# First attention of a two-block model: 32 written-out rounds with the compressed branch and the turning of heads in pieces between them, first queries staged early

## The reference, cut to what matters

```python
def nsa_attention(q, gates, k_cmp, v_cmp, k_sel, v_sel, k_win, v_win, rel_bias):
    ...
        logit_c = jnp.einsum('bqghd,bngd->bqghn', qt, k_cmp) + bias_c[None]   # 31 compressed blocks
        p_c = jax.nn.softmax(logit_c, axis=-1) * has_any[...]
        o_c = jnp.einsum('bqghn,bngd->bqghd', p_c, v_cmp)
        ...
        logit_s = jnp.einsum('bqghd,bqgkd->bqghk', qt, ks) + bias_s           # selected blocks
        ...
        logit_w = jnp.einsum('bqghd,bkgd->bqghk', qt, kw) + bias_w[None]      # window of 512
        ...
        o = gt[..., 0:1] * o_c + gt[..., 1:2] * o_s + gt[..., 2:3] * o_w
    ...
def nsa_mixer(h, w_qg, w_o, shared, rel_bias):
    ...
    return o.reshape(B, S, N_HEADS * HEAD_DIM) @ w_o
```

## Time and profile before

| | |
|---|---|
| median of 3 runs | 2545.89 us (2544.61 to 2548.26) |
| the profiled execution's own time | 2548.19 us |
| its span, first to last instruction | 2546.3 us |
| PE busy | 2435.9 us (96%) |
| DVE busy | 1550.6 us (61%) |
| ACT busy | 875.4 us (34%) |
| POOL busy | 60.2 us (2%) |
| mean granted PE clock | 0.978 of 2.4 GHz |
| chain that ended last | PE 86%, DVE 7%, issue 4%, ACT 2%, DMA 1% |

### The profile page before, as it was taken

How to read it: one execution, slowest core, us unless ns; L and a number is a source line. 1 busy time by engine, 2 the same in 40 slices (tenths; PEclk the granted TensorE clock), 3 DMA queues, 4 the chain that set the end, 5 groups by cost and what they waited for, 6 DMA issues and landing times.

```text
span 2546.3 us, 38807 instructions
## 1 busy us (share of the span) xinstructions
PE 2435.9 (96%) x14805; PEld 2141.5 (84%) x14805; DVE 1550.6 (61%) x2803; ACT 875.4 (34%) x1343; POOL 60.2 (2%) x55
## 2 busy tenths in 40 slices
PE   6999999999989899999999989998998999999998
PEld 4888888888878788888878889988997999997996
DVE  5556444456477756344468875876665655884784
ACT  3123222234344443222244761673332333222222
POOL 0000000000112000000000000000100000000000
PEclk9999999999989899999999999999999999999999
DMA  4236224324433002222223422431221122223223
GB/s 141 89 99 149 88 99 144 122 99 126 150 104 71 21 29 92 91 100 96 86 99 101 122 63 84 118 100 67 83 83 65 64 84 84 83 99 128 87 84 115
DMA packets 91769, 242.42 MB, mean 95 GB/s; under 512 B 24886, under 2 KB 58166, under 8 KB 67638
## 3 DMA queue, kind: packets, MB, share of 16 engines
q1 hardware_dynamic: 29056, 198.26, 21.6%
q10 hardware_dynamic: 60808, 36.42, 6.4%
q0 software_dynamic: 1760, 5.77, 1.0%
HBM read 230.51 MB, written 11.14 MB: 95 GB/s over the span
## 4 chain that ended last, share of the span: by engine, by line
PE 86%; DVE 7%; issue 4%; ACT 2%; DMA 1%; ACTq 0%; DVEq 0%
PE ps L972 42%; PE ps L1208 24%; PE ps L1461 4%; PE ps L1309 3%; PE ps L1161 3%; PE ps L1106 1%; PE ps L1144 1%; DVE wlo L1478 1%; PE ps L1394 1%; PE ps L1065 1%; PE ps L1368 1%; DMA buckets<-in_buckets 1%; PE ps L992 1%; PE ps L1133 1%; ACT L L817 1%
## 5 line engine op out<-in xcount | busy, mean ns | idle before, releaser
L522 ACT ACTIVATE whi<-raw 128x2048 fp32r<-128x2048 f32 x187 | 357.6, 1912 | 731.9 <-PE ps L972 495.1
L1478 DVE TENSOR_TENSOR wlo<-raw,whi 128x2048 fp32r<-128x2048 f32 (+1 forms) x207 | 430.6, 2080 | 66.1 <-ACT whi L522 65.2
L972 PE MATMUL ps<-parts,whi 128*128 128x512 f32 x1360 | 429.7, 397 | 0.0
L1208 PE MATMUL ps<-parts,whi 128*128 128x264 f32 (+1 forms) x2400 | 409.9, 293 | 10.9 <-DVE sq L2109 5.6
L1208 PEld LDWEIGHTS ps<-parts,whi 128*128 128x128 f32 x2400 | 335.1, 191 | 22.7 <-issue 16.9
L972 PEld LDWEIGHTS ps<-parts,whi 128*128 128x128 f32 x1360 | 255.9, 189 | 62.1 <-issue 1.6
L972 PE MATMUL ps<-parts,wlo 128*128 128x512 f32 x680 | 269.4, 396 | 0.0
L1208 PE MATMUL ps<-parts,wlo 128*128 128x264 f32 (+1 forms) x1200 | 244.0, 285 | 0.0
L972 PE MATMUL ps<-Mhi,whi 128*128 128x512 f32 x512 | 203.0, 396 | 0.0
L972 PE MATMUL ps<-Mlo,whi 128*128 128x512 f32 x512 | 203.0, 396 | 0.0
L972 PE MATMUL ps<-Mhi,wlo 128*128 128x512 f32 x512 | 203.0, 396 | 0.0
(11 more groups left out here) (363 smaller groups left out, 3921.0 us busy)
## 6 DMA issues: line engine op xcount, KB each, us to landing
raw<-in_stream SPq DMA_DIRECT2D x187, 1024.0 KB, 4.8
bands<-scratch ACTq DMA_DIRECT2D x8, 1024.0 KB
csb<-sums_d ACTq DMA_DIRECT2D x16, 512.0 KB, 5.7
near<-bands ACTq DMA_DIRECT2D x20, 256.0 KB, 2.6
csf<-sums_d ACTq DMA_DIRECT2D x32, 128.0 KB, 6.0
Qst<-parts POOLq DMA_DIRECT2D x14, 256.0 KB, 6.1
tabs<-bands ACTq DMA_DIRECT2D x8, 418.0 KB, 4.2
X<-in_x SPq DMA_DIRECT2D x4, 512.0 KB, 16.6
```

The source lines that it names most:

```text
L522: nc.scalar.activation(whi[:, s, :], raw[:, s, :], ACT.Copy).then_inc(hi_done, 1)
L972: mm = nc.tensor.matmul(out, w[:, s, at], x(k), start=k + j == 0, stop=k == k_tiles - 1 and j == 2)
L1208: mm = nc.tensor.matmul(ps[:, 2 * par + h, 0:w], wt[:, s, at], x[:, k, a + h * w:a + (h + 1) * w], start=k + j == 0, stop=k == k_tiles - 1 ...
L1478: low = nc.vector.tensor_tensor(wlo[:, s, a:b], raw[:, s, a:b], whi[:, s, a:b].bitcast(F32), ALU.subtract)
```

## The change

- `ROUNDS` is 8 and the three loops of two iterations are gone: 32 rounds are written out (`n`, with group `g = n // 8` and `r = n % 8`), with constant waits and addresses.
- In round n PE does `turn(n)`, `scores(n + 2)`, then `beside_round(n)`, then `values(n)`. `beside_round` waits for `weighted(n - 1)` (`ov_done`, n) and does one piece in the bank of 6 and 7 that is free, `6 + (n + 1) % 2`: r = 0 the turning of the last two heads of the group before, r = 1 the second half of this group's compressed values, r = 2 and 3 the next group's compressed scores, a half each, r = 4 the turning of the first two heads, r = 5 the turning of the next group's compressed probabilities, r = 6 the first half of its values. `values(n + 1)` waits until the piece has been read.
- DVE does its part of each piece between `scores(n + 2)` and `weighted(n)`; ACT its part after its copy of turned probabilities. The last two heads of the last group are turned inside the first output unit, in front of its second tile.
- Compressed keys are formed behind unit `q2`; the values after `scores(0)`; the compressed scores of group 0 come ahead of `scores(0)`.
- For group 0, ACT copies the first two query tiles ahead of its split of the q3 weights and issues the high half at once; POOL issues the low half after two subtractions, not five. DVE's subtraction of the q3 weights comes ahead of the other query tiles; that of the phi3 weights in two halves in rounds 7 and 15.
- `Qst` and `Ks` are two tensors each (even and odd groups), and the order of tensors in SBUF changes. `bands` loses the four extra heads (1 MB written in `mlp0`) and `near` is loaded 16 times in place of 20, three of the first four loads later.

```diff
-ROUNDS = 2 * HPG * 2
+ROUNDS = 2 * HPG
+ALL_ROUNDS = GROUPS * ROUNDS
...
             stage_keys(0)
-            pool.wait_ge(q_lo, KT - 3)
+            pool.wait_ge(q_lo, 2)
             stage_queries(pool, 0, q_staged[0], (1,))
...
             for c in range(4):
+                if c == 3:
+                    act.wait_ge(mt_full, T0["q3"] + 2)
+                    query_high(0)
+                    query_high(1)
+                    act.wait_ge(q_hi, 2)
+                    stage_queries(act, 0, q_first, (0,))
                 next_unit(f"q{c}", 0)
...
                 if c == 3:
                     query_high(KT - 2)
                     query_high(KT - 1)
-                    act.wait_ge(q_lo, KT - 3)
-                    stage_queries(act, 0, q_first, (0,))
+                    for n in range(1, HPG):
+                        load_near(n, 0)
                     next_unit(f"phi{c}", 0, m=1)
...
+            nc.scalar.activation(spare[:, :], vec("eps"), ACT.Exp)
...
+            for n in range(ALL_ROUNDS):
+                g, r = divmod(n, ROUNDS)
+                act.wait_ge(pt_full, n + 1)
+                nc.scalar.activation(PT[:, 0:SEQ], ps[:, 3, :], ACT.Copy).then_inc(pt_act, 1)
+                if r == 0 and g:
+                    heads_high(g - 1, 1)
+                if r == 4:
+                    heads_high(g, 0)
+                    if g < GROUPS - 1:
+                        compressed_exp(g + 1)
+                if n + 2 < ALL_ROUNDS:
+                    exps(n + 2)
...
+            def beside_round(n):
+                g, r = divmod(n, ROUNDS)
+                last = g == GROUPS - 1
+                if n:
+                    pe.wait_ge(ov_done, n)
+                bank = 6 + (n + 1) % 2
+                if r == 0 and g:
+                    heads_turned(g - 1, 1, bank)
+                if r == 1:
+                    compressed_values(g, 1, bank)
+                if r in (2, 3) and not last:
+                    compressed_scores(g + 1, r - 2, bank)
+                if r == 4:
+                    heads_turned(g, 0, bank)
+                if r == 5 and not last:
+                    compressed_turned(g + 1, bank)
+                if r == 6 and not last:
+                    compressed_values(g + 1, 0, bank)
...
+            compressed_scores(0, 0, 6)
+            compressed_scores(0, 1, 7)
+            pe.wait_ge(mt_free, T0["phi3"] + 1)
+            scores(0)
+            compressed_blocks()
+            compressed_turned(0, 7)
+            scores(1)
+            pe.wait_ge(cmp_ready, 2)
+            compressed_values(0, 0, 6)
+            for n in range(ALL_ROUNDS):
+                turn(n)
+                if n + 2 < ALL_ROUNDS:
+                    scores(n + 2)
+                beside_round(n)
+                values(n)
...
             for c in range(4):
-                unit("o", c, H1, ready=(lambda k: (o_ready, k + 1)) if not c else None)
+                unit("o", c, H1, ready=(lambda k: (o_ready, k + 1)) if not c else None, beside={} if c else {(1, 0): last_heads})
...
+            compressed_in(0, 0, 6)
+            compressed_in(0, 1, 7)
+            compressed_max(0)
+            scores(0)
+            values_compressed()
+            dve.wait_ge(cmp_ready, 2)
+            compressed_turned(0, 7)
+            scores(1)
+            compressed_coefs(0)
+            compressed_out(0, 0, 6)
+            for n in range(ALL_ROUNDS):
+                g, r = divmod(n, ROUNDS)
+                last = g == GROUPS - 1
+                bank = 6 + (n + 1) % 2
+                coefs(n)
+                turned(n)
+                if n + 2 < ALL_ROUNDS:
+                    scores(n + 2)
+                if r == 0 and g:
+                    heads_low(g - 1, 1)
+                if r == 1:
+                    compressed_out(g, 1, bank)
+                if r in (2, 3) and not last:
+                    compressed_in(g + 1, r - 2, bank)
+                if r == 3 and not last:
+                    compressed_max(g + 1)
+                if r == 4:
+                    heads_low(g, 0)
+                    if not last:
+                        compressed_coefs(g + 1)
+                if r == 5 and not last:
+                    compressed_turned(g + 1, bank)
+                if r == 6 and not last:
+                    compressed_out(g + 1, 0, bank)
+                if r == 7 and g < 2:
+                    split_low("phi3", 0, part=g)
+                weighted(n)
+            heads_low(GROUPS - 1, 1)
```

More of the change, by code:

```diff
@@ L727, in _ @@
                     next_unit(f"phi{c}", 0, m=1)
-                for k in range(KT - 2 if c == 3 else 0):
+                for k in range(2, KT - 2 if c == 3 else 0):
                     query_high(k)
@@ L779, in _ @@
+            heads_high(GROUPS - 1, 1)
             for c in range(4):
@@ new lines, in compressed_scores @@
+            def compressed_scores(g, half, bank):
+                if not half:
+                    pe.wait_ge(cmp_ready, 1)
+                    queries_staged(g)
+                for h in (half, half + 2):
+                    for t in range(QT):
+                        at = (h // 2 * QT + t) * 2 * CMP_PAD
+                        mm = nc.tensor.matmul(ps[:, bank, at:at + 2 * CMP_PAD], Qst[g % 2][:, h, t * P:(t + 1) * P], kch[:, g, :], start=True, stop=True)
+                mm.then_inc(cs_full, 1)
@@ new lines, in values @@
+            def values(n):
+                g, r = divmod(n, ROUNDS)
+                if n >= 2:
+                    pe.wait_ge(ov_done, n - 1)
+                if n:
+                    beside_read(n - 1)
+                else:
+                    pe.wait_ge(co_done, 1)
+                for k in (0, 1, 3, 2):
+                    if k == 0:
+                        pe.wait_ge(pt_act, n + 1)
+                    else:
+                        pe.wait_ge(pt_dve, 2 * n + (2 if k == 2 else 1))
+                    for t in range(k, QT):
+                        at = KEYS_AT[k] + (t - k) * P
+                        mm = nc.tensor.matmul(ps[:, 6 + n % 2, t * DH:(t + 1) * DH], PT[:, at:at + P], Vt[:, n % 2, k, g * DH:(g + 1) * DH],
+                                              start=k + t == 0, stop=k == 2 and t == 3, skip_group_check=True)
+                mm.then_inc(ov_full, 1)
@@ L1725, in _ @@
                     nc.vector.tensor_scalar(seen, seen, vec("has_any"), None, ALU.mult).then_inc(gate_ready, 1)
-                if c < 3:
-                    split_low(f"q{c}", 0)
-                for k in range(KT - 3 if c == 3 else 0):
+                if c == 2:
+                    dve.wait_ge(cmp_full, 1)
+                    keys = ps[:, 4, 0:GROUPS * CMP_PAD].rearrange("p (g n) -> p g n", g=GROUPS)
+                    own.mark(nc.vector.tensor_scalar(kch[:, :, 0:CMP_PAD], keys, one, None, ALU.mult))
+                    own.wait()
+                    nc.vector.tensor_tensor(kch[:, :, CMP_PAD:], keys, kch[:, :, 0:CMP_PAD].bitcast(F32), ALU.subtract).then_inc(cmp_ready, 1)
+                if c == 3:
+                    query_low(0)
+                    query_low(1)
+                split_low(f"q{c}", 0)
+                for k in range(2, KT - 3 if c == 3 else 0):
                     query_low(k)
@@ L1854, in _, with values_compressed, scores @@
-            for h in range(HPG):
-                dve.wait_ge(near_loaded[h], 16 * (GROUPS + 1))
+            def values_compressed():
+                dve.wait_ge(cmp_full, 2)
+                own.mark(nc.vector.tensor_copy(vcmp[:, :], ps[:, 5, 0:GROUPS * DH]))
+                own.wait()
+                for t in range(QT):
+                    copy = nc.vector.tensor_scalar(vcs[:, t, :], vcmp[:, :], vec("quarter", t), None, ALU.mult)
+                copy.then_inc(cmp_ready, 1)
+            def scores(n):
+                g, r = divmod(n, ROUNDS)
+                if r % 2 == 0:
+                    dve.wait_ge(near_loaded[r // 2], 16 * (g + 1))
+                dve.wait_ge(s_full, n + 1)
+                own.mark(nc.vector.memset(step[:, :], 0.0))
+                for t in range(QT):
+                    bank, at = ((0, 0), (1, 0), (0, P), (2, 0))[t]
+                    w = (t + 1) * P
+                    nc.vector.tensor_tensor_reduce(Sb[:, n % 2, first(t):first(t) + w], ps[:, bank, at:at + w], near[:, r // 2, SEQ - w:SEQ],
+                                                   -1.0, -2 * MASKED, ALU.add, ALU.min, nmax[:, n % 2, t:t + 1]).then_inc(ttr_done, 1)
@@ new lines, in coefs, with turned @@
+            def coefs(n):
+                g, r = divmod(n, ROUNDS)
+                dve.wait_ge(exp_done, 4 * n + 4)
+                own.mark(nc.vector.reciprocal(rsum[:, n % 2, :], rsum[:, n % 2, :]))
+                own.wait()
+                own.mark(nc.vector.tensor_tensor(coef[:, n % 2, :], rsum[:, n % 2, :], gates[:, :, 3 * (g * HPG + r // 2) + 1 + r % 2], ALU.mult))
+            def turned(n):
+                dve.wait_ge(pt_full, n + 1)
```

(14 more changed lines are left out.)

406 lines of the change are left out of this document (156 added, 250 removed).

## The result

| | before | after |
|---|---|---|
| median of 4 runs each | 2545.25 us (2541.72 to 2548.26) | 2506.86 us (2505.01 to 2507.65) |
| ratio, 95% interval | | 0.9843 (0.9831 to 0.9855) |
| profiled execution: own time, span | 2548.19, 2546.3 us | 2507.65, 2505.8 us |
| PE busy, DVE busy | 2435.9, 1550.6 us | 2414.6, 1546.3 us |
| mean granted PE clock | 0.978 | 0.989 |

The change saves 38.4 us by the medians, 1.5% (1.6% by the ratio); 33.1 were foretold, and a time of 2513.0. Two later measurements of the same kernel, on two chips, gave 2508.32 and 2508.04, just inside it. Mechanism and sign came out; the gain was forecast 5.3 us too small, and where those lie is the question of this part.

What follows compares the result with a forecast made beforehand. TensorE was taken to bound the rounds, with passages between them neither dense nor at full clock. Gains of 27.8 us behind round 1 and 5.3 at the start made 33.1: 2545.9 to 2512.8, predicted 2513, range 2507 to 2523.

Steps and rivals of the forecast that it cites:

- 158.3: Round 1 to the first output unit: forecast us after the change, against 186.1 before, a gain of 27.8.
- stalls: Round 5 of a group: TensorE waits for VectorE, 0.43 us a group, 1.3 in all; bounds 0 and 1.2 a group.
- the 0.5 of GpSimd's keys in rounds 5 and 6: Rounds 5 and 6: GpSimd's key staging for groups 2 and 3 adds 0.5 us, from 0 to 4.
- near 897: Sign that the forecast is right: the time in us at which the output unit starts, 929.84 before.
- The start: Ahead of round 1: earlier first queries let round 1 start at 738.4 instead of 743.75, a gain of 5.3 us.
- value products 1.75, turning 2.0, scores 2.7, values 2.5: Start, behind the copy of turned values at 729.1: TensorE's steps at half clock, so round 1 starts at 738.0.
- the bounds of the start and of the stalls: Start gain 2.7 at worst to 7.7 at best; round 5 stalls from 0 to 1.2 us a group.
- VectorE sets the pace: Rival for the rounds: hand-overs and rounds 3 to 5 cost more; gain 23.6, time 2522.3; chance 0.10.
- The lock: Rival, groups 2 and 3: four GpSimd key operations each hold a VectorE operation; gain 26.0, 2519.9 us; chance 0.06.
- The start gives nothing: Rival: VectorE's chain from 719.9 is the longer one at the start; gain 27.8, time 2518.1; chance 0.12.
- Passages come back as waits: Rival: passages return as waits inside the rounds, so nothing overlaps as said; gain some 12, time 2534; chance 0.04.
- Slower: Rival: TensorE waits every round for weighted(n-1); loss passes gain if VectorE's rounds average over 6.3 us; chance 0.02.

Runs made afterwards that it cites:

- Experiment 10: The changed kernel with one more VectorE product of two SBUF operands (128x512) in each of the 32 rounds; 2518.04 us, ratio 0.9885.
- experiment 11: The changed kernel with the next group's compressed branch in one block behind round 6's scores instead of one piece a round; 2537.51 us, ratio 0.9959.
- experiment 5: The changed kernel with GpSimd's key staging of group 1 held until VectorE's four value scalings are done; 2509.59 us, ratio 0.9860.

## Where the prediction was right, and what failed

**Right.** Rounds without a piece take 4.55 us, those with half of the scores or values 5.42 to 5.45; TensorE is busy without a gap from round 1 to the last two rounds, at full clock, and the one round that is longer than its products is round 5. The pace was TensorE's, as said, and VectorE kept up: from round 1 to the unit 157.4 us with the turnings inside it, against 158.3. That is 0.9 less, mostly in two terms: stalls were 0.18 a group and not 0.43, and no round is longer for the 0.5 of GpSimd's keys in rounds 5 and 6. Its operations fell beside VectorE's reads of PSUM and one product of 128x4, which took 0.36 us in place of 0.17. Experiment 10 shows what they would have cost beside a 128x512 product of two SBUF operands.

The output unit came at 892.56, not near 897. Of these 4.1 us, 1.1 is this execution's earlier arrival at `phi3`, 0.85 the moved work, 0.9 the rounds just told, and 1.3 the start.

**The start was mis-sized: 5.3, measured 6.6.** The steps up to the copy of the turned values were right to half a us: first product 716.5, measured 715.2 where the whole execution runs 1.1 earlier; the scalings held by GpSimd, to 728.3 as foretold and to 727.6 as measured. What failed is the step behind it, "value products 1.75, turning 2.0, scores 2.7, values 2.5" at half clock. It takes 735.58 - 728.45 = 7.13 us in place of 8.95: the clock fell only within the value products and came back in round 0's scores. I had put the whole round at the lower level.

**The base was one execution: 3 us.** The sum was made against one profile of the kernel before, with its own passages at their own clock: "From the start of round 1 to that point the kernel takes 929.84 - 743.75 = 186.1 us". In two others it is 187.7 and 187.8, and the start 1.4 longer. What the change takes away is just the part whose length moves from one profile to the next. Against the mean of the two others the gain is 225.1 - 186.2 = 39.0 less 0.85 for the moved work, 38.1, where the medians say 38.4. Against the mean of all three it is 37.1, and which length is the usual one three profiles don't tell. The agreement with 38.4 is in part luck, too: the unchanged code behind the stage also differs by some us between profiles, and on the later chips the medians stand 38.9 and 39.8 apart. I had said that this profile's own time was 2.3 above the median, and taken that as harmless; it was a short attention and a long scan together.

**The range** took in the bounds of the start and of the stalls, but nothing for the base. With 3 us for it its low end would have been 2504. The miss of 0.14 us is less than what the kernel's own medians move (2506.86, 2508.04, 2508.32), so it is the 5.3 us that teach something, not the 0.14.

**The rivals.** VectorE sets the pace: no; experiment 10 shows that even 0.68 us more a round costs 1 us a group without GpSimd. The lock: present, but it costs in the start and not in rounds 5 and 6. The start gives nothing: no. Passages come back as waits: this is experiment 11, where it cost 30 us. Slower: no round came near its 6.3 us.

## What to carry to other kernels

A short serial passage in a TensorE-bound stage costs its waits and can cost the half clock behind them, in experiment 11 about as much again (5.5 us of waits, 10.2 in all); a single wait, such as the 1.48 us in experiment 10, left the clock up. Spread it over the rounds, one piece each, in the engine's own order, and give each piece a round of slack for its reader. And before a passage is priced from a profile, look at a second execution of the same kernel: here the part that is partly at half clock differed by 3 us between them, where the dense part agreed to hundredths.

## What the runs showed that I had not expected

- The clock's fall is not tied to one wait. Behind the same waits of 0.69 and 0.21 us, one execution of the kernel before ran round 14's last products and the turning behind them at the higher level, and two others, later and both on one chip, ran them at the lower.
- GpSimd's key operations lengthen some VectorE operations that stand beside them: products of two SBUF operands (2.00 us for 0.19, 1.88 for 0.17, 2.95 for 0.68) and the scalings of one SBUF tensor by a value per partition (3.69 for 1.14). Others they leave as they are: a reciprocal beside them took its 0.25 us at 728.03 in experiment 5, and the additions of bias, which read PSUM, their 0.69. Moving the key operations in the start moved the loss with them; the two other orders of the start gave 2507.74 and 2509.59 us, neither better than the changed kernel.
